# A diffusion trunk on one core: attention's low query parts on GpSimd and its normalisation per row of tiles, transposes of the experts at the ends of chunk groups, last sums in another order

## The chip, the cores and the metric

The kernel runs on one core of one Trainium2 chip. The metric is the device time of one launch in microseconds. Three runs of the kernel before gave 3383.38, 3388.33 and 3390.08 us; the median is 3388.33 us.

## What is computed

One trunk layer is applied to two groups of rows, 256 prompt rows and 1024 sample rows of width 1024, with shared weights. Cut to what matters here:

```python
def trunk_layer(x, cond, attend, ...):
    h = rmsnorm(x, norm1_g) * (1.0 + sc1) + sh1
    q, k, v, hy = jnp.split(h @ w_in, ...)
    a = attend(to_heads(q) * (HEAD_DIM ** -0.5), k, v)      # 8 heads of 64
    y_h = hyena_mixer(hy, conv_w, conv_b, k_f, hy_bias)
    mix = concat(rmsnorm(a, out_g_attn), rmsnorm(y_h, out_g_hyena)) @ w_out
    x = x + g1 * mix
    h2 = rmsnorm(x, norm2_g) * (1.0 + sc2) + sh2
    return x + g2 * expert_choice_ffn(h2, w_router, w1, w3, w2)   # 16 experts, ff 2816
y = rmsnorm(x, final_g)
```

Prompt rows attend to all 256 prompt keys. Sample rows lie on a 16 x 64 grid and attend, in one softmax, to a window of 8 x 16 neighbours with a relative bias and to 256 cached keys. Each expert takes its 128 best sample rows and its 32 best prompt rows (128 columns of 4 quarters in the second projection), computes silu(x w1) * (x w3), multiplies by w2, scales by the gate and adds the rows to x. All data is 32 bits wide.

## The kernel before, in words

The program is a row of phases, each with its own block of five engine programs written out by hand; nothing is scheduled automatically. Engines are ordered by semaphores, so the order in which each engine's code stands is the order in which it runs. The phases are filters, projection (`projection`), attention (`attention`), hyena, mixing and routing, and experts (`experts`).

**Split operands.** Matrices for samples are split in two parts, a rounded high part (ScalarE, a copy with rounding) and the rest as a low part. In attention the 64 rows of a head's queries are loaded twice, on partitions 0 to 63 and 64 to 127. ScalarE's `query_high` scales all 128 partitions by 1/8 and rounds (L802), and VectorE's `query_low` puts the rest on partitions 64 to 127 (L734). Keys are split by ScalarE (L795, L797) and GpSimd (L625, L627).

**Attention.** There are 8 heads of 10 tiles of 128 queries: tiles 0 and 1 are prompts, 2 to 9 windows, 80 tiles in all. For tile n, TensorE issues `scores(n + 1)` (L642, L646, L652), `transposes(n)` of the probabilities (L660, L669), and `values(n - 1)` (L688) into the one bank `po`. VectorE runs `add_max(n + 1)` (L746 or L748 and L750), `copy_ctx(n)` (L757), `norm(n - 1)` (a reciprocal of the sum in column 64 of `po`, L762, and a multiply, L764), and, behind tiles 6 and 7 of every head but the last, one half of the next head's `query_low`. ScalarE runs `copy_win(n)` (L820) and `exps(n + 1)` (L809, L813), and between them the high parts of the next head. `values(n)` waits for `s_norm`, that is until `norm(n - 1)` has emptied `po`. Behind the last head TensorE transposes `ar` tile by tile (`out_transposes`, L698), ScalarE and VectorE copy the banks out by turns, and two DMAs write `MIXT` (L616). ScalarE also takes the sum of squares of each tile of `ar` (`square`, L826).

**Experts.** An expert has 66 weight chunks of 512 KB. Chunks 0 to 43 (w1 and w3) make six units, five of 8 chunks and a narrow one (40 to 43); chunks 44 to 65 are w2. For each group of chunks TensorE first does `samples(c)` for every chunk of the group, with split operands and three matmuls for each product (L2806 to L2808), and then `prompts(c)` for the same chunks (L2816), in strips of 32 columns of the array. The groups end at chunks 7, 15, 23, 31, 39, 43, 51, 58 and 65. After the samples of the chunks that `TURN` names, it transposes the hidden rows of an earlier unit (L2788, L2790: six transposes, three for the last unit), and after chunk `X_TURN` the next expert's rows (L2774, L2778: ten). Two chunks later in their own loops, ScalarE and VectorE split what was transposed (`hid_hi`, L2601 and L2602, and `hid_lo`, L2670). VectorE also makes the low part of every chunk (L2500), three chunks ahead. In the last expert both engines also norm and scale the ten row tiles that only wait for their output (`bulk_square`, `bulk_first`, `bulk_scale`).

**The end.** The rows of the last expert are gathered once more, VectorE adds the last expert's output to the samples' rows `xg` and the prompts' quarters `xq`, ScalarE takes the squares, TensorE sums the quarters' squares (L2845), VectorE and ScalarE form the inverse roots, and GpSimd scatters both to `y` (L2574, L2576).

```python
    TURN = {11: 0, 19: 1, 27: 2, 35: 3, 43: 4, 47: 5}
    X_TURN = 55
```

## Time and profile before

| | us |
|---|---|
| median of three runs | 3388.33 |
| the profiled execution's own time | 3388.24 |
| its span | 3386.5 |
| TensorE busy in the span | 3194.2 (94%) |
| VectorE busy | 2191.4 (65%) |
| ScalarE busy | 1655.8 (49%) |
| GpSimd busy | 382.8 (11%) |
| attention, from the first split of keys to the last square | 680.5 to 886.9 |
| experts' matmuls | about 1336 to 3367 |

The span is the time between the first and the last instruction that the profiler saw; 1.7 us of the execution lie around it. A busy share is an average over phases with different limits, so each part of the change is read in its own stretch of the timeline.

### The profile page before, as it was taken

Reading aid. Unit: us, or ns where it says so; the run is one execution under the profiler, and the core shown is the slowest. Engines: PE = TensorE matmul, PEld = TensorE weight load, DVE = VectorE, ACT = ScalarE, POOL = GpSimd, SP = SyncE. Lnnn points to the kernel's source line nnn. Section 1 sums busy time; section 2 is a strip of 40 time slices with the busy share of each in tenths; the row PEclk is TensorE's granted clock in tenths of the full one; section 3 lists DMA queues with packets and bytes.
Section 4 is the critical chain, followed back from the end, with each engine's and each line's share of the span. In section 5 each row is a group of like instructions: output and inputs, shape, how many; then the busy total and the mean of one; then the engine's idle time right before and its main releaser. Section 6 shows DMA issues by size and latency. Waiting matters only on the chain.

```text
span 3386.5 us, 54111 instructions
## 1 busy us (share of the span) xinstructions
PE 3194.2 (94%) x22270; PEld 2430.6 (72%) x22270; DVE 2191.4 (65%) x2815; ACT 1655.8 (49%) x2156; POOL 382.8 (11%) x319
## 2 busy tenths in 40 slices
PE   5997999979899894999999999999999999999997
PEld 2443888878778773777777777777777777777775
DVE  7644233167666547777777777777777777777767
ACT  1103222156411323666666666666666666666665
POOL 2210100011244131000000000000000000000010
PEclk8998999989999896999999999999999999999999
DMA  5464432254676434788778777777777778777786
GB/s 175 170 228 177 116 115 84 73 143 127 230 245 216 149 100 162 278 297 295 272 288 294 274 288 292 275 288 290 274 290 292 275 287 295 270 289 294 275 316 247
DMA packets 226035, 791.14 MB, mean 234 GB/s; under 512 B 28526, under 2 KB 35322, under 8 KB 221565
## 3 DMA queue, kind: packets, MB, share of 16 engines
q1 hardware_dynamic: 206028, 722.02, 57.6%
q0 software_dynamic: 19760, 65.65, 6.8%
q8 instruction: 177, 2.90, 0.3%
q14 instruction: 70, 0.57, 0.0%
HBM read 730.31 MB, written 57.26 MB: 233 GB/s over the span
## 4 chain that ended last, share of the span: by engine, by line
PE 58%; DVE 1%; DMA 1%; ACT 0%; issue 0%; POOL 0%; SPq 0%; ACTq 0%; POOLq 0%; DVEq 0%
PE exp_bank L2806 15%; PE exp_bank L2808 14%; PE exp_bank L2807 14%; PE exp_bank L2816 14%; PE exp_bank L2788 1%; DMA exp_xb<-residual 1%; PE exp_bank L2790 1%; PE exp_bank L2774 0%; DMA out_y<-exp_xb 0%; DVE exp_lo L2500 0%; DVE g_pick L2367 0%; DVE g_pick L2366 0%; DVE g_pick L2369 0%; DVE exp_xb L2714 0%; DMA exp_xq<-hidden_rows,g_rows_q 0%
## 5 line engine op out<-in xcount | busy, mean ns | idle before, releaser
L2500 DVE TENSOR_TENSOR exp_lo<-exp_raw,exp_hi 128x1024 fp32r<-128x1024 f32 x1056 | 1277.8, 1223 | 249.7 <-ACT exp_hi L2496 190.8
L2496 ACT ACTIVATE exp_hi<-exp_raw 128x1024 fp32r<-128x1024 f32 x1056 | 1119.1, 1061 | 570.8 <-PE exp_bank L2808 556.7
L2806 PE MATMUL exp_bank<-exp_hi,exp_xt 128*128 128x512 f32 (+1 forms) x1536 | 588.6, 383 | 1.3 <-DVE exp_xt L2655 1.0
L2808 PE MATMUL exp_bank<-exp_hi,exp_xt 128*128 128x512 f32 (+1 forms) x1536 | 572.0, 372 | 0.0
L2807 PE MATMUL exp_bank<-exp_lo,exp_xt 128*128 128x512 f32 (+1 forms) x1536 | 571.7, 372 | 0.0
L2806 PEld LDWEIGHTS exp_bank<-exp_hi,exp_xt 128*128 128x128 f32 x1536 | 289.6, 189 | 87.0 <-issue 39.1
L2808 PEld LDWEIGHTS exp_bank<-exp_hi,exp_xt 128*128 128x128 f32 x1536 | 289.7, 189 | 51.9
L2816 PE MATMUL exp_bank<-exp_raw,exp_xtp 128*32 128x256 f32 (+1 forms) x6144 | 324.1, 363 | 0.0
L2807 PEld LDWEIGHTS exp_bank<-exp_lo,exp_xt 128*128 128x128 f32 x1536 | 290.2, 189 | 45.4
L2806 PE MATMUL exp_bank<-exp_hi,exp_hid 128*128 128x512 f32 x704 | 282.8, 402 | 0.7 <-DVE exp_lo L2500 0.7
L2816 PEld LDWEIGHTS exp_bank<-exp_raw,exp_xtp 128*32 128x32 f32 x6144 | 185.1, 110 | 127.0 <-issue 30.8
L2808 PE MATMUL exp_bank<-exp_hi,exp_hid 128*128 128x512 f32 x704 | 274.9, 390 | 0.0
L2807 PE MATMUL exp_bank<-exp_lo,exp_hid 128*128 128x512 f32 x704 | 274.3, 390 | 0.0
L503 PE MATMUL proj_bank<-proj_hh,proj_hi 128*128 128x512 f32 (+1 forms) x480 | 170.6, 355 | 2.0 <-DVE proj_lo L126 2.0
L504 PE MATMUL proj_bank<-proj_hl,proj_hi 128*128 128x512 f32 (+1 forms) x480 | 170.6, 356 | 0.0
L505 PE MATMUL proj_bank<-proj_hh,proj_lo 128*128 128x512 f32 (+1 forms) x480 | 170.5, 355 | 0.0
L2547 POOL TENSOR_TENSOR exp_step<-g_ident 1x1 f32<-1x1 f32 x16 | 4.0, 250 | 1422.8 <-PE exp_bank L2778 1391.6
L2806 PEld LDWEIGHTS exp_bank<-exp_hi,exp_hid 128*128 128x128 f32 x704 | 132.2, 188 | 42.5 <-issue 15.9
L2816 PE MATMUL exp_bank<-exp_raw,exp_hidp 128*32 128x256 f32 x2816 | 161.9, 381 | 0.0
L2808 PEld LDWEIGHTS exp_bank<-exp_hi,exp_hid 128*128 128x128 f32 x704 | 132.1, 188 | 28.6
L2807 PEld LDWEIGHTS exp_bank<-exp_lo,exp_hid 128*128 128x128 f32 x704 | 132.4, 188 | 25.2
L1180 PE MATMUL filt_pk<-filt_opnd,filt_table 128*128 128x512 f32 x292 | 140.1, 622 | 5.3 <-DVE filt_spec L1408 5.2
(413 smaller groups left out, 4299.1 us busy)
## 6 DMA issues: line engine op xcount, KB each, us to landing
exp_raw<-in_w SPq DMA_DIRECT2D x1056, 512.0 KB
hy_table<-in_basis_s POOLq DMA_DIRECT2D x64, 512.0 KB
carry_tiles<-in_w_ada SPq DMA_DIRECT2D x24, 1024.0 KB, 5.5
proj_raw<-in_w_in SPq DMA_DIRECT2D x24, 512.0 KB
filt_table<-in_kbasis_s SPq DMA_DIRECT2D x18, 512.0 KB, 6.1
spectrum_s<-filt_spec SPq DMA_DIRECT2D x34, 256.0 KB, 2.2
carry_flex<-spectrum_s SPq DMA_DIRECT2D x16, 512.0 KB
features<-proj_xr SPq DMA_DIRECT2D x12, 512.0 KB, 3.0
```

The costliest lines, as they stand in the source:

```text
L503: pe.matmul(out, whi, hh[:, k, c0:c0 + w], start=(k == 0), stop=False)
L504: pe.matmul(out, whi, hl[:, k, c0:c0 + w], start=False, stop=False)
L505: mm = pe.matmul(out, wlo, hh[:, k, c0:c0 + w], start=False, stop=(k == KT - 1))
L1180: mm = pe.matmul(pk[n % 2][:], table[:, c % NR, ti * 128:(ti + 1) * 128], opnd[:, at, x, :], start=(t == 0), stop=(t == nt - 1 and not rank1))
L2496: act.activation(st.hi[:, n % st.ns, :], raw(n), ACT.Copy).then_inc(st.hi_done, 1)
L2500: dve.tensor_tensor(st.lo[:, n % st.ns, :], raw(n), st.hi[:, n % st.ns, :].bitcast(F32), ALU.subtract).then_inc(st.lo_done, 1)
L2788: pe.transpose(turn_s[:, i * 128:(i + 1) * 128], hd[:, i * 128:(i + 1) * 128], g["ident"][:])
L2790: tr = pe.transpose(turn_p[:, i * 128:(i + 1) * 128], hdp[:, i * 128:(i + 1) * 128], g["ident"][:])
L2806: pe.matmul(out, xh, wh, start=(k == 0), stop=False)
L2807: pe.matmul(out, xh, wl, start=False, stop=False)
L2808: mm = pe.matmul(out, xl, wh, start=False, stop=(k == nk - 1))
L2816: mm = pe.matmul(banks(e * NU + i)[2][q * CAP_P:(q + 1) * CAP_P, 0:w], x[:, k, :], raw(e * NC + c)[:, base + q * w:base + q * w + w], star ...
```

## The change

In attention, the factor 1/8 moves into the projection's copies of the query blocks. VectorE's `query_low` goes, and GpSimd does the same subtraction behind its keys. `norm` becomes `copy_out`: one copy of all 65 columns of `po` into `raw_o`. In the last head, VectorE inverts the 8 sums of a tile at once and GpSimd multiplies the tile's 512 columns. The squares come one tile later. In the experts, `TURN` and `X_TURN` name the last chunks of groups. At the end, the samples' sums and squares stand ahead of the wait for the prompts' matmuls, and the inverse root is formed twice, for samples first.

```diff
@@ projection, ScalarE and VectorE
-                        ins = act.activation(to, part, ACT.Copy)
+                        ins = act.activation(to, part, ACT.Copy, scale=HD ** -0.5 if QK_ORDER[m] < 4 else 1.0)
...
+                    if QK_ORDER[m] < 4:
+                        ins = dve.tensor_scalar(to, part, HD ** -0.5, None, ALU.mult)
+                    else:
+                        ins = dve.tensor_copy(to, part)
@@ attention, GpSimd
             for h in range(NH):
                 u = h % 2
+                if h:
+                    pool.wait_ge(s_ql, 2 * h)
                 for x, (c0, c1) in enumerate(KP):
                     pool.wait_ge(s_kh, 3 * h + x + 1)
                     pool.tensor_tensor(kl[:, u, c0:c1], k[u][:, c0:c1], kh[:, u, c0:c1].bitcast(F32), ALU.subtract).then_inc(s_kl, 1)
...
+                pool.wait_ge(s_kl, 3 * h + 3)
+                for x, (c0, c1) in enumerate(KP):
+                    pool.wait_ge(s_qh, 2 * h + x + 1)
+                    out = qs[64:128, u, c0:c1]
+                    pool.tensor_tensor(out, q[u][64:128, c0:c1], out.bitcast(F32), ALU.subtract).then_inc(s_ql, 1)
+            pool.wait_ge(s_ql, 2 * NH)
+            for t in range(NTT):
+                pool.wait_ge(s_li, t + 1)
+                pool.tensor_tensor(ar[:, t, :].rearrange("p (h d) -> p h d", h=NH), raw_o[:, t, :, 0:HD],
+                                   li[:, t, :].rearrange("p (h o) -> p h o", o=1).to_broadcast([128, NH, HD]),
+                                   ALU.mult).then_inc(s_norm, 1)
@@ attention, TensorE: values(n) and out_transposes(t)
-                    pe.wait_ge(s_norm, n)
+                    pe.wait_ge(s_po, n)
...
-                pe.wait_ge(s_norm, NT - NTT + t + 1)
+                pe.wait_ge(s_norm, t + 1)
@@ attention, VectorE
-            def norm(n):
+            def copy_out(n):
                 h, t = TILES[n]
                 dve.wait_ge(s_pv, n + 1)
-                dve.reciprocal(li[:, n % 2:n % 2 + 1], po[:, HD:HV]).then_inc(s_li, 1)
-                dve.wait_ge(s_li, n + 1)
-                dve.tensor_scalar(ar[:, t, h * HD:(h + 1) * HD], po[:, 0:HD], li[:, n % 2:n % 2 + 1], None,
-                                  ALU.mult).then_inc(s_norm, 1)
+                dve.tensor_copy(raw_o[:, t, h, :], po[:, 0:HV]).then_inc(s_po, 1)
+                if h == NH - 1:
+                    dve.wait_ge(s_po, n + 1)
+                    dve.reciprocal(li[:, t, :], raw_o[:, t, :, HD]).then_inc(s_li, 1)
...
-                if h + 1 < NH and t in (6, 7):
-                    query_low(h + 1, t - 6)
@@ attention, ScalarE
-                elif t >= 2:
-                    square(t - 2)
+                elif t >= 3:
+                    square(t - 3)
@@ experts
-    TURN = {11: 0, 19: 1, 27: 2, 35: 3, 43: 4, 47: 5}
+    TURN = {15: 0, 23: 1, 31: 2, 39: 3, 43: 4, 51: 5}
...
-    X_TURN = 55
+    X_TURN = 58
@@ experts, ScalarE
-            for x in (2, 0, 1):
+            for x in range(3):
                 last_square(x)
-            act.wait_ge(s_lroot, 1)
-            act.activation(lroot[:], lr2[:], ACT.Sqrt).then_inc(s_lroot, 1)
+            for x in range(2):
+                act.wait_ge(s_lroot, 2 * x + 1)
+                act.activation(lroot[:, x:x + 1], lr2[:, x:x + 1], ACT.Sqrt).then_inc(s_lroot, 1)
@@ experts, VectorE
-            prompt_done(dve, LAST, NB)
+            done(dve, LAST, NB)
             dve.wait_ge(s_xr, 32)
             dve.wait_ge(s_bss, NTT)
-            y_part(LAST, 2).then_inc(s_lstep, 1)
             for x in range(2):
                 y_part(LAST, x).then_inc(s_lstep, 1)
-            dve.wait_ge(s_lstep, 1)
-            dve.tensor_tensor(xq[:], xq[:], yq[:], ALU.add).then_inc(s_lx, 1)
...
+            prompt_done(dve, LAST, NB)
+            y_part(LAST, 2).then_inc(s_lstep, 1)
+            dve.wait_ge(s_lstep, 3)
+            dve.tensor_tensor(xq[:], xq[:], yq[:], ALU.add).then_inc(s_lx, 1)
@@ experts, TensorE
-            pe.wait_ge(s_lss, 1)
+            pe.wait_ge(s_lss, 3)
```

VectorE in the middle of a head of attention, tiles 5 to 7, before (`attn_nc` is the context maximum, `attn_pt` the probabilities, `attn_po` the bank of values):

```order
L757 COPY attn_pt<-attn_ptc 128x256
L762 RECIPROCAL attn_li<-attn_po 128x1
L764 TENSOR_SCALAR attn_ar<-attn_po,attn_li 128x64
L734 SCALAR_TENSOR_TENSOR attn_qs<-carry_tiles,attn_qs 64x640
L748 TENSOR_REDUCE attn_nc<-attn_psc 128x1
L750 ISA attn_sw,attn_nm<-attn_psw,attn_bias,attn_nc 128x384
L750 ISA attn_nm 128x1
```

and the same place now:

```order
L766 COPY attn_pt<-attn_ptc 128x256
L771 COPY attn_raw_o<-attn_po 128x65
L757 TENSOR_REDUCE attn_nc<-attn_psc 128x1
L759 ISA attn_sw,attn_nm<-attn_psw,attn_bias,attn_nc 128x384
L759 ISA attn_nm 128x1
```

One copy stands where a reciprocal and a multiply stood, and the query rows no longer stand between one tile's output and the next tile's maximum.

TensorE in the first expert, around the transposes of the first unit's hidden rows (`exp_hd`, `exp_hdp`), before:

```order
L2807 MATMUL exp_bank<-exp_lo,exp_xt 128x512
L2808 MATMUL exp_bank<-exp_hi,exp_xt 128x512
L2788 MATMUL exp_bank<-g_ident,exp_hd 128x128 x4
L2790 MATMUL exp_bank<-g_ident,exp_hdp 128x128 x2
L2806 MATMUL exp_bank<-exp_hi,exp_xt 128x512
```

and now:

```order
L2820 MATMUL exp_bank<-exp_lo,exp_xt 128x512
L2821 MATMUL exp_bank<-exp_hi,exp_xt 128x512
L2801 MATMUL exp_bank<-g_ident,exp_hd 128x128 x4
L2803 MATMUL exp_bank<-g_ident,exp_hdp 128x128 x2
L2829 MATMUL exp_bank<-exp_raw,exp_xtp 32x256 x32
```

The transposes stood between two chunks of samples and now stand between the last chunk of samples and the prompts' matmuls of the group. Only the narrow unit's end had them there before.

VectorE at the end of the program, before (`exp_ys` and `exp_xg` are the samples' rows, `exp_yq` and `exp_xq` the prompts' quarters):

```order
L2677 SCALAR_TENSOR_TENSOR exp_yq<-exp_bank,g_gate_q,exp_row_q 128x256
L2676 SCALAR_TENSOR_TENSOR exp_ys<-exp_bank,g_gate_s,exp_row_s 128x512 x2
L2748 TENSOR_TENSOR exp_xq<-exp_xq,exp_yq 128x256
L2752 TENSOR_TENSOR exp_xg<-exp_xg,exp_ys 128x512 x2
L2755 TENSOR_TENSOR exp_lrr<-exp_lss 128x1
```

and now:

```order
L2682 SCALAR_TENSOR_TENSOR exp_ys<-exp_bank,g_gate_s,exp_row_s 128x512 x2
L2755 TENSOR_TENSOR exp_xg<-exp_xg,exp_ys 128x512 x2
L2683 SCALAR_TENSOR_TENSOR exp_yq<-exp_bank,g_gate_q,exp_row_q 128x256
L2759 TENSOR_TENSOR exp_xq<-exp_xq,exp_yq 128x256
L2769 TENSOR_TENSOR exp_lrr<-exp_lss 128x1
```

The samples' two rows stood behind the wait for the prompts' matmuls and now stand ahead of it.

## Rows read from the trace of the kernel before

**Rows 1.** Windows view, all of core 0: window, length, engines busy (instructions), PE clock, DMA.

```profile
720.00:760.00 40.00, 38.67 (x298) 34.52 (x298) 31.84 (x103) 27.05 (x56) 7.65 (x6) 1.00 0.50 133
...
1400.00:1800.00 400.00, 400.00 (x3230) 305.32 (x3230) 292.28 (x282) 252.54 (x294) 23.77 (x18) 1.00 0.77 287
```

**Rows 2.** Timeline: VectorE's copies of context columns, tiles 6 and 8, third and last head.

```profile
756.88 0.42 DVE L757 COPY attn_pt<-attn_ptc 128x256 f32<-128x256 f32 x1
...
762.57 0.42 DVE L757 COPY attn_pt<-attn_ptc 128x256 f32<-128x256 f32 x1
...
872.22 0.42 DVE L757 COPY attn_pt<-attn_ptc 128x256 f32<-128x256 f32 x1
...
876.75 0.42 DVE L757 COPY attn_pt<-attn_ptc 128x256 f32<-128x256 f32 x1
```

**Rows 3.** Timeline, third head and the turn to the fourth: start, length (us), engine, line.

```profile
755.11 0.61 ACT L813 ACTIVATE attn_p<-attn_sw,attn_nm 128x384 f32<-128x384 f32 x1
...
755.90 0.49 PE L669 MATMUL attn_ptw<-g_ident,attn_p 128*128 128x128 f32 x3
...
758.01 0.82 DVE L734 SCALAR_TENSOR_TENSOR attn_qs<-attn_q,attn_qs 64x640 fp32r<-64x640 f32 x1
...
766.00 0.63 PE L688 MATMUL attn_po<-attn_vc,attn_pt 128*128 128x65 f32 x4 [0.16 <-DVE attn_ar L764]
```

**Rows 4.** Timeline, first head's start, and GpSimd beside VectorE in the third head.

```profile
682.82 3.48 DVE L734 SCALAR_TENSOR_TENSOR attn_qs<-carry_tiles,attn_qs 64x640 fp32r<-64x640 f32 x2 [2.19 <-ACT attn_qs L802]
...
684.32 1.30 POOL L627 TENSOR_TENSOR attn_ckl<-carry_tiles,attn_ckh 128x256 fp32r<-128x256 f32 x1
...
700.30 0.74 ACT L795 ACTIVATE attn_kh<-attn_k 128x640 fp32r<-128x640 f32 x1 [6.25 <-DMA attn_bias<-in_bias]
...
751.70 1.54 POOL L625 TENSOR_TENSOR attn_kl<-attn_k,attn_kh 128x640 fp32r<-128x640 f32 x1 [0.44 <-ACT attn_kh L795]
...
751.82 0.62 DVE L750 CUSTOM_DVE_ANT_0 attn_sw<-attn_psw,carry_tiles,attn_nc 128x384 f32<-128x384 f32 x1
```

**Rows 5.** Timeline, end of attention; then the DMA view's issue row (median us to landing).

```profile
882.46 0.17 DVE L762 RECIPROCAL attn_li<-attn_po 128x1 f32<-128x1 f32 x1 [0.37 <-PE attn_po L688]
...
884.64 0.60 PE L698 MATMUL attn_psc<-g_ident,attn_ar 128*128 128x128 f32 x4
...
mixed<-attn_at SPq DMA_DIRECT2D x1, 1024.0 KB, 6.2
```

**Rows 6.** Timeline of TensorE, sixth expert: third unit, then the narrow unit's end.

```profile
2006.86 0.39 PE L2808 MATMUL exp_bank<-exp_hi,exp_xt 128*128 128x512 f32 x1
...
2009.58 0.39 PE L2808 MATMUL exp_bank<-exp_hi,exp_xt 128*128 128x512 f32 x1
...
2012.98 0.39 PE L2808 MATMUL exp_bank<-exp_hi,exp_xt 128*128 128x512 f32 x1
...
2013.30 1.07 PE L2816 MATMUL exp_bank<-exp_raw,exp_xtp 128*32 128x256 f32 x16
...
2053.94 0.38 PE L2790 MATMUL exp_bank<-g_ident,exp_hdp 128*128 128x128 f32 x2
...
2054.25 0.54 PE L2816 MATMUL exp_bank<-exp_raw,exp_xtp 128*32 128x128 f32 x12
```

**Rows 7.** Timeline of TensorE, last expert, second projection.

```profile
3349.03 0.50 PE L2806 MATMUL exp_bank<-exp_hi,exp_hid 128*128 128x512 f32 x1 [0.68 <-DVE exp_lo L2500]
```

**Rows 8.** Chain that ended last, in order of time, at the program's end.

```profile
3367.31 1.32 DVE exp_ys L2676 x2
...
3368.96 1.21 DVE exp_xg L2752 x2
...
3370.70 1.23 ACT exp_ys L2618 x4
...
3373.65 1.30 DVE exp_xg L2761
...
3377.13 0.99 POOL out_y L2576
```

More of the change, by code:

```diff
@@ L546, in attention @@
         nc0, nm = ph.sb("nc0", [128, 2]), ph.sb("nm", [128, 2])
-        li = ph.sb("li", [128, 2])
+        li = ph.sb("li", [128, NTT, NH])
+        raw_o = ph.sb("raw_o", [128, NTT, NH, HV])
         ar = ph.sb("ar", [128, NTT, DA])
@@ L727, in _ @@
             dve.memset(vc[:, :, :, HD:HV], 1.0).then_inc(s_one, 1)
-            def query_low(h, x):
-                u = h % 2
-                dve.wait_ge(s_qh, 2 * h + x + 1)
-                c0, c1 = KP[x]
-                out = qs[64:128, u, c0:c1]
-                dve.scalar_tensor_tensor(out, q[u][64:128, c0:c1], HD ** -0.5, out.bitcast(F32),
-                                         ALU.mult, ALU.subtract).then_inc(s_ql, 1)
             def add_max(n):
@@ L775, in _ @@
                 if n:
-                    norm(n - 1)
-                if h + 1 < NH and t in (6, 7):
-                    query_low(h + 1, t - 6)
+                    copy_out(n - 1)
             for t in range(1, NTT, 2):
                 if t == 5:
-                    norm(NT - 1)
+                    copy_out(NT - 1)
                 dve.wait_ge(s_tr, t + 1)
@@ L801, in query_high @@
                 c0, c1 = KP[x]
-                act.activation(qs[:, u, c0:c1], q[u][:, c0:c1], ACT.Copy, scale=HD ** -0.5).then_inc(s_qh, 1)
+                act.activation(qs[:, u, c0:c1], q[u][:, c0:c1], ACT.Copy).then_inc(s_qh, 1)
             def exps(n):
@@ L847, in _ @@
                 act.activation(at_out(t), at_in(t), ACT.Copy).then_inc(s_ata, 1)
-            for t in range(NTT - 2, NTT):
+            for t in range(NTT - 3, NTT):
                 square(t)
```

25 lines of the change are left out of this document (13 added, 12 removed).

## The prediction

> **What bounds the kernel now.** I read the windows view first. In the experts, from 1400 to 1800 us, TensorE is busy for 400.00 of 400 us at the full granted clock of 1.00 (2.4 GHz), and no other engine comes near that. In attention, from 720 to 760 us, it is busy for 38.67 of 40 us, VectorE for 31.84 and GpSimd for 7.65 [rows 1]. So the experts can only gain if TensorE's own stream gets shorter, and attention can only gain where TensorE stands still. The timeline shows where that is [rows 2, 3]. The chain of waits, last, gives the end of the program, where TensorE has finished and the other engines work in single file [rows 8]. The sum is made against the profiled execution's 3388.24 us, which is the median of the runs (3388.33) to within 0.1 us.
>
> **Attention: the query subtraction leaves VectorE.** The reader is to compare two stretches of equal work. From the copy of tile 6 to that of tile 8 it takes 762.57 - 756.88 = 5.69 us in the third head, where two halves of `query_low` of 0.82 us each [rows 3] stand between, and 876.75 - 872.22 = 4.53 us in the last head, which has none [rows 2]. The difference is 1.16 us. It is less than 1.64 because VectorE is not full. Seven heads have it: 7 x 1.16 = 8.1 us. Part of it comes back at once. Behind the last window tile the next scores are a prompt tile's: 768 columns less, at 0.227 us for 512 [rows 6] 0.34 us less, by which the transposes come earlier. In an undisturbed tile the window exponentials end at 755.72 and their transposes start at 755.90 [rows 3], 0.18 us of slack, so about 0.15 us is waited for at each turn: 7 x 0.15 = 1.0 us. Net gain 7.1 us.
>
> **Attention: one copy in place of `norm`.** In a window tile TensorE waits for nothing, so nothing is gained. At the turn from one head to the next, `values` of the last window tile waits for `norm` of the one before; TensorE starts at 766.00 behind VectorE's multiply [rows 3]. The reciprocal takes 0.17 us [rows 5]; with the handing over it adds about 0.2. A copy of 65 columns does not stand in the trace. It lies between 0.17 us (one column) and 0.42 us (256 columns, [rows 2]); I take 0.25, nearer to the one column. The wait gets shorter by 0.17 us at each of 7 turns: 1.2 us. If the copy cost 0.42, this would be nothing; if all of the wait went, 2.3 us. The waits behind it (for the maximum of the first window tile, and for its exponentials) start from TensorE's scores and stay.
>
> **Attention: the same work on GpSimd.** GpSimd takes 1.54 us for 128x640 [rows 4]. A half of 64 partitions has as many columns, so I take 1.55 us; the bounds are 0.8 (half) and 2.2. In a running head ScalarE makes the high query rows behind tiles 5 and 6. GpSimd can begin there, a tile (2.26 us) ahead of where VectorE began, and takes 0.73 us longer, so it ends 1.5 us earlier than VectorE did: nothing. At the start of the first head it is serial: cached keys from 684.32 for 0.6 to 0.8 us, then 3.1 us for the queries, about 688.2 instead of 682.82 + 3.48 = 686.30 for VectorE [rows 4]. These 1.9 us are covered: ScalarE stands still for 6.25 us until 700.30 for a DMA of the second head [rows 4], and that DMA doesn't wait for the queries. If that cover were gone, it would cost 1.9 us. The loads of the third head, which do wait for them, go out about 1 us later and leave the second head's more room: 0 to 0.7 us of gain, taken as 0.
>
> **Attention: the multiply on GpSimd.** Ten multiplies of 128x512 come with the last head. By the ratio of columns one takes 1.54 x 512 / 640 = 1.25 us; for the broadcast operand I let it be up to twice that. They come every 2.26 us, so they keep up. The last one decides: its values are there at 882.46 [rows 5]; copy, reciprocal and multiply end near 884.4. Its transposes started at 884.64, held by a bank [rows 5]. So 0, and up to 1.2 us if the multiply takes twice as long, passed straight to the DMA of 6.2 us [rows 5] that ends the phase. The three squares behind the copies end near 887.8, under that DMA. The factor 1/8 changes no instruction count in the projection, whose copies lie under matmuls: nothing, and if that cover were gone still under 0.1 us each for 12 blocks.
>
> **Experts: the transposes.** TensorE's starts tell the price. In steady samples one matmul takes (2012.98 - 2009.58) / 15 = 0.227 us. From 2006.86 to 2009.58 [rows 6] lie nine matmuls and six transposes of 0.11 us: 2.70 us without any cost of switching, against 2.72 measured. So a place in the middle of samples costs 0.02 to 0.03 us beyond the transposes themselves. Where samples turn to prompts, the start of prompts comes 0.32 us after the last sample matmul [rows 6], 0.09 more than 0.227. Where transposes stand between them, the second of the last two stands at 2054.05 and prompts start at 2054.25, 0.20 us or 0.09 more than 0.11 [rows 6]. The price of turning to strips is thus the same with and without transposes in front. The move saves only the 0.02 to 0.03: 4 x 16 of six transposes, 16 of three and 15 of ten are 95 places, and 95 x 0.025 = 2.4 us. The bounds are 0 and, if the 0.09 were hidden too, 95 x 0.11 = 10.5 us. The Trainium skill says in "TensorEngine Tiling (Array Packing)", section Key Properties, that a change of the tiling mode drains TensorE; transposes use the whole array as samples do, so by that rule no such change goes away and the sum would have 0 here instead of 2.4.
>
> **Experts: the last one.** The low part of the last unit's hidden rows is now made behind the bulk rows' root chain, not ahead of it. Just there TensorE waits for a low part of weights, 0.68 us until 3349.03 [rows 7]. ScalarE's high part and VectorE's low part, 0.6 to 0.7 us together, come on top. I take 0.7 us of loss; bounds 0 and 1.5. The other 15 experts have no such wait.
>
> **The end.** Today two output parts (1.32 us), two additions (1.21) and two squares (1.23) of the samples [rows 8] stand behind the last prompts' matmul. They now run beside the last seven chunks' matmuls for prompts, 56 records; by 16 records in 1.07 us, the last of them 0.38 long in the model [rows 6], that is about 3 us, and ScalarE's squares overlap VectorE's additions. That takes off 3.76 us. The samples' sum, scale and reciprocal steps then run beside the square of the quarters, another 0.5 us. Multiplying the samples' rows (at 3373.65) thus comes about 4.3 us earlier. The second root chain costs about 1.6 us (the joint one took 3373.65 - 3371.93 = 1.72) and the quarters' multiply some 0.5 (256 of the 1024 columns that take 1.30, and the fixed part), 2.1 us behind the first one. Today the second scatter starts at 3377.13, 2.18 us after that multiply's end at 3374.95 [rows 8], because the first scatter is issued between. So the second chain just fits under it. Gain 4.3 us; bounds 3.3 (the chain is 1 us late) and 4.8.
>
> **Sum.** -7.1 - 1.2 - 2.4 + 0.7 - 4.3 = -14.3 us, so 3388.24 - 14.3 = 3373.9; I give 3374.
>
> **Rivals.** *The transposes are worth more.* If the start of prompts were hidden behind them, the 10.5 us bound would replace 2.4: 3366. The equal 0.09 us in both rows speak against it. Chance 0.09. *GpSimd is slower than by columns, or the head's turn eats more of the gain.* With 1.2 us lost at the end of attention and only half of the 7.1 us kept: 3388.2 - 3.6 - 1.2 - 2.4 + 0.7 - 4.3 + 1.2 = 3379. The maximum, exponential and transposes are a ring behind every tile, which speaks for it; the undisturbed last head speaks against. Chance 0.15. *The move to GpSimd does not come into effect:* if the low query rows were late for each head by the 1.2 us that VectorE lost, only the end and the small terms remain: 3381. GpSimd would have to take about 3 us for each half. Chance 0.05. *GpSimd locks VectorE out; slower.* At the start, VectorE took 3.48 us for two halves of 0.82 and GpSimd 1.30 for its 256 columns [rows 4], because they ran together. If GpSimd blocked VectorE in attention too, each of 14 halves and 10 multiplies would stop it for up to 1.5 us: 14 x 1.55 + 10 x 1.25 = 34 us, less 14.3, gives 3408; from about 0.6 us for each operation on, the gain is gone. Against it: from 751.70 GpSimd worked for 1.54 us, and VectorE's operation at 751.82 took its usual 0.62 [rows 4]; it reads PSUM and one SBUF operand. The Trainium skill agrees ("SBUF — State Buffer", section Who interferes with whom): VectorE contends if it has two SBUF inputs or a two-port mode. By that rule nothing of the 34 us would come, since attention has no such operation on VectorE now; the trace at 682.82 and at 751.82 agrees. Chance 0.04.
>
> **How the numbers follow.** My forecast has 0.67. The terms at their best ends (8.1 + 2.3 + 2.4 + 0.7 + 4.8 = 18.3 us, no loss in the last expert) give 3370. All at their worst at once (half of 7.1 and 3.3 gained, 1.5 and 1.2 lost) would give 3384, but that needs four misses in one direction; the second and third rival lie at 3379 and 3381. The three runs lie within 7 us of each other, so the lower end goes to 3368. The range is 3368 to 3381; it leaves out the first and the last rival, 0.13, and the edges of the others. A measurement tells 0.2%, 6.8 us, from no change, so faster means under 3381.5: 0.87. Within 0.2%: 0.09, a part of the second and third rival. Slower: 0.04.
>
> **What would show it.** VectorE's rows in attention should be a copy of about 0.25 us in place of two instructions, and each of the first seven heads should take about 1.2 us less, end to end. TensorE's first wait of attention gets longer by about 2 us and ScalarE's wait until about 700 shorter by as much. In the experts the starts from sample to transposes to prompts should be 0.227, 0.11 and 0.20. The samples' additions should stand before the last prompts' matmul ends. A VectorE operation of attention above its old length, a GpSimd half above 2.2 us, or a TensorE wait for a low part of weights in experts 0 to 14 would prove me wrong.

## The result and the profile after

The changed kernel takes 3369.36 us (median of five runs, 3363.19 to 3372.25) beside 3383.77 us for the kernel before in the same session (3383.38 to 3390.08). The medians are 14.4 us apart. The ratio is formed from all runs: it is 0.9949, with a 95% interval of 0.9938 to 0.9959, which is 17.3 us less (13.9 to 21.0). A second session with the same kernel gave 0.9959 (0.9946 to 0.9973), 13.9 us less. The forecast was 14.3 us less. The change is faster, as predicted. The totals can't tell whether it gives more than forecast, since 14.3 lies in both intervals; the stretches below tell that attention does. One run of all that are reported here, 6212.7 us of turn_only, was in a slow state and stands in no ratio.

Single executions of one kernel differ by up to 15 us here, so the account is drawn up from the traces, stretch by stretch. Both profiled executions are used with their own time: 3388.24 us before and 3371.65 us after, 16.6 us less.

| stretch | before | after | difference | predicted |
|---|---|---|---|---|
| up to attention's first split of keys (changed only by the factor 1/8) | 680.49 | 679.81 | -0.68 | 0 |
| from there to the last copy of transposed rows | 205.47 | 196.12 | -9.35 | -8.3 |
| between attention and experts (unchanged code) | 449.96 | 449.87 | -0.09 | 0 |
| experts, first sample matmul to last prompts' matmul | 2030.83 | 2028.75 | -2.08 | -1.7 |
| from there to the end of the span | 19.70 | 15.31 | -4.39 | -4.3 |

The factor 1/8 costs nothing that shows: the projection's matmuls take 361.09 us before and 361.12 after, first start to last end.

The windows view of the changed kernel answers to [rows 1]. Its columns are window, length, and the busy time of TensorE, its weight loads, VectorE, ScalarE and GpSimd, then the granted clock and DMA:

```profile
720.00:760.00 40.00, 39.05 (x311) 35.78 (x310) 28.08 (x88) 29.04 (x59) 13.87 (x10) 1.00 0.48 122
1400.00:1800.00 400.00, 400.00 (x3288) 308.17 (x3281) 295.23 (x284) 252.18 (x297) 23.78 (x18) 1.00 0.78 288
```

In attention VectorE has gone from 31.84 to 28.08 us of 40 and GpSimd from 7.65 to 13.87. TensorE stands still 0.95 us instead of 1.33, while more heads' work goes through. In the experts TensorE is busy all the time, as before, and gets more done: 3288 matmuls instead of 3230 fall in the same 400 us (some records are missing, so this is a sign, and the periods below are the measure).

**A running head.** The timeline of VectorE in the changed kernel shows the copies of context columns. The first and last rows are tile 0 of the third and of the fourth head; the two between are tiles 6 and 8 of the third:

```profile
740.21 0.41 DVE L766 COPY attn_pt<-attn_ptc 128x256 f32<-128x256 f32 x1
...
753.90 0.42 DVE L766 COPY attn_pt<-attn_ptc 128x256 f32<-128x256 f32 x1
...
758.43 0.42 DVE L766 COPY attn_pt<-attn_ptc 128x256 f32<-128x256 f32 x1
...
761.86 0.41 DVE L766 COPY attn_pt<-attn_ptc 128x256 f32<-128x256 f32 x1
```

A head takes 761.86 - 740.21 = 21.65 us. Before, the same two copies stood in the timeline at

```profile
743.02 0.41 DVE L757 COPY attn_pt<-attn_ptc 128x256 f32<-128x256 f32 x1
...
766.10 0.42 DVE L757 COPY attn_pt<-attn_ptc 128x256 f32<-128x256 f32 x1
```

so 23.08 us: 1.4 us less for each head (1.41 on the mean of six). From tile 6 to tile 8 it now takes 758.43 - 753.90 = 4.53 us, exactly what the last head took in [rows 2].

**VectorE beside GpSimd.** GpSimd's low query half and the four VectorE instructions beside it, from the timeline of the changed kernel:

```profile
753.36 0.62 DVE L759 CUSTOM_DVE_ANT_0 attn_sw<-attn_psw,carry_tiles,attn_nc 128x384 f32<-128x384 f32 x1
753.50 1.56 POOL L638 TENSOR_TENSOR attn_qs<-attn_q,attn_qs 64x640 fp32r<-64x640 f32 x1 [1.91 <-ACT attn_qs L807]
753.90 0.08 DVE L759 DVE_READ_ACCUMULATOR2_ANT attn_nm<- 128x1 f32 x1
753.90 0.42 DVE L766 COPY attn_pt<-attn_ptc 128x256 f32<-128x256 f32 x1
754.51 0.23 DVE L771 COPY attn_raw_o<-attn_po 128x65 f32<-128x65 f32 x1 [0.19 <-PE attn_po L705]
```

The low query half takes 1.56 us on GpSimd, and the four VectorE instructions beside it have the lengths they have alone: 0.62 and 0.42 us, as in [rows 4] and [rows 2]. The copy of 65 columns takes 0.23 us.

**The start.** GpSimd's keys and queries run one behind the other, and TensorE waits for them:

```profile
680.63 3.04 POOL L631 TENSOR_TENSOR attn_kl<-carry_tiles,attn_kh 128x640 fp32r<-128x640 f32 x2 [247.30 <-ACT attn_kh L800]
...
683.64 0.71 POOL L633 TENSOR_TENSOR attn_ckl<-carry_tiles,attn_ckh 128x256 fp32r<-128x256 f32 x1
684.43 3.02 POOL L638 TENSOR_TENSOR attn_qs<-carry_tiles,attn_qs 64x640 fp32r<-64x640 f32 x2
687.50 0.29 PEld L659 LDWEIGHTS attn_psc<-attn_kh,attn_qs 128*128 128x128 f32 x1 [13.67 <-POOL attn_qs L638]
...
700.72 0.74 ACT L800 ACTIVATE attn_kh<-attn_k 128x640 fp32r<-128x640 f32 x1 [5.02 <-DMA attn_bias<-in_bias]
```

The first scores start 7.69 us after the first split of keys, against 5.86 before: 1.83 us later. ScalarE's wait for the second head's load [rows 4] is now 5.02 us instead of 6.25.

**The end of attention.** Groups of the changed kernel by line, between 673 and 876 us (busy us, mean ns of one, idle before):

```profile
L771 DVE COPY attn_raw_o<-attn_po 128x65 f32<-128x65 f32 x80 | 18.0, 224 | 29.1 <-PE attn_po L705 29.1
...
L642 POOL TENSOR_TENSOR attn_ar<-attn_raw_o,attn_li 128x512 f32<-128x512 f32 x10 | 10.4, 1045 | 19.7 <-DVE attn_li L774 19.7
```

A multiply takes 1.05 us and waits for VectorE before every one, never the other way.

**The experts.** TensorE where samples end in the sixth expert, from the timeline:

```profile
2000.87 0.39 PE L2821 MATMUL exp_bank<-exp_hi,exp_xt 128*128 128x512 f32 x1
2001.11 0.60 PE L2801 MATMUL exp_bank<-g_ident,exp_hd 128*128 128x128 f32 x4
2001.54 0.38 PE L2803 MATMUL exp_bank<-g_ident,exp_hdp 128*128 128x128 f32 x2
2001.85 1.93 PE L2829 MATMUL exp_bank<-exp_raw,exp_xtp 128*32 128x256 f32 x32
```

Prompts start 0.31 us after the first of the last two transposes, which is 0.20 after the second. That is the same as at the narrow unit's end in [rows 6]. An expert takes 126.56 us instead of 126.74.

**The end.** The chain that ended last, in order of time (start, us, what), answers to [rows 8]:

```profile
3351.39 3.20 PE exp_bank L2829 x56
...
3354.61 0.49 DVE exp_yq L2683
...
3355.13 0.43 DVE exp_xq L2759
...
3355.59 0.51 ACT exp_yq L2625 x2
...
3357.05 1.29 DVE exp_xg L2771
...
3359.84 0.49 DVE exp_xq L2775
3360.33 0.27 issue
3360.60 0.99 POOL out_y L2581
```

Ahead of the two root chains only the quarters' part, their addition and their squares stand behind the prompts' matmul now. The samples' parts and additions lie under it, in VectorE's timeline:

```profile
3351.43 1.41 DVE L2682 SCALAR_TENSOR_TENSOR exp_ys<-exp_bank,g_gate_s,exp_row_s 128x512 f32<-128x512 f32 x2 [1.93 <-PE exp_bank L2821]
3352.75 1.28 DVE L2755 TENSOR_TENSOR exp_xg<-exp_xg,exp_ys 128x512 f32<-128x512 f32 x2
```

### The profile page after: what moved, and what is told of

Same layout as the page of the kernel before. It is cut to its first block, busy times and chain, and to the rows that moved or that the text cites. A ratio compares the mean times of both kernels' runs of the same rounds, so it can differ in the third digit from the quotient of the medians.

```text
span 3369.9 us, 54074 instructions
## 1 busy us (share of the span) xinstructions
PE 3182.6 (94%) x22270; PEld 2439.4 (72%) x22270; DVE 2179.3 (65%) x2735; ACT 1657.9 (49%) x2157; POOL 417.7 (12%) x345
## 4 chain that ended last, share of the span: by engine, by line
PE 58%; DVE 1%; DMA 1%; ACT 0%; issue 0%; POOL 0%; SPq 0%; ACTq 0%; DVEq 0%
PE exp_bank L2819 15%; PE exp_bank L2821 14%; PE exp_bank L2820 14%; PE exp_bank L2829 14%; PE exp_bank L2801 1%; DMA exp_xb<-residual 1%; PE exp_bank L2803 1%; PE exp_bank L2787 0%; DMA out_y<-exp_xb 0%; DVE exp_lo L2505 0%; DVE g_pick L2372 0%; DVE g_pick L2371 0%; DVE g_pick L2374 0%; DVE exp_xb L2720 0%; ACT exp_hi L2501 0%
```

## The experiments

Twelve experiments ran. Where single runs scatter by more than the question is worth, the answer is taken from the stretch of the trace.

**attn_only**: projection and attention of the change, the experts and the end of before.

> Only the projection's scaling and attention are changed. My theory (terms add up, each in its own stretch): the part of attention gives 9 to 10 us in the trace (first split of keys to the last copy of the transposed rows), nothing else moves, 3374 to 3375 against 3384. Rival (attention's gain is partly given back later, at the phase's end or by the next phase's start): under 6 us. Rival (the later phases are worth more than their rows say): under 7 us here and over 10 in the other two runs.

Measured: 0.9968 (0.9956 to 0.9980). Attention took 196.10 us, 9.37 less than before, a head 21.65 us, an expert 126.74, the end 19.70. The theory's 9 to 10 us hold. So attention's gain is all its own, and it is 1.1 us more than the prediction's 8.3.

**turn_only**: only the places of the transposes.

```diff
-    TURN = {11: 0, 19: 1, 27: 2, 35: 3, 43: 4, 47: 5}
+    TURN = {15: 0, 23: 1, 31: 2, 39: 3, 43: 4, 51: 5}
...
-    X_TURN = 55
+    X_TURN = 58
```

> Only the places of the transposes in the experts are changed. My theory: 0.025 us for each of 95 places less 0.7 to 1.0 in the last expert, 1.5 to 2.5 us less, all between the first and the last matmul of the experts, and starts of sample, transposes and prompts at 0.227, 0.11 and 0.20 us. Rival (the turn to strips is hidden behind the transposes): 8 to 10 us less. Rival (nothing, since no change of the array's mode goes away): within 0.5 us.

Measured: 1.0002 (0.9993 to 1.0012). The total shows nothing: a gain of 2 us lies within its interval, -2.4 to 4.1 us. (In the profiled execution the first head of attention, unchanged code, took 37.56 us instead of 31.05.) The trace does show the gain: an expert takes 126.56 us instead of 126.74, and all of the experts take 1.42 us less, just under the 1.5 that the theory had as its least. If the 0.09 us of turning to strips were hidden too, an expert would have to be 0.66 us shorter (10.5 / 16). It is 0.18 shorter, so that rival is out.

**tail_only**: only the new order at the end.

> Only the order at the end is changed. My theory: 4.3 to 4.4 us less, all behind the last prompts' matmul, and the second scatter starts right behind the first. Rival (the second root chain is not hidden): 2.5 to 3.3 us less, with an idle GpSimd between the two scatters.

Measured: 0.9989 (0.9980 to 0.9998), and the end took 15.31 us instead of 19.70: all of the 4.39 us, with nothing else changed. The scatters start 1.37 us apart here too, so the part of the theory that had the second one right behind the first missed by 0.06 us.

**whole_again**: the changed kernel once more, beside the three parts.

> The changed kernel once more, on the chip and beside the runs of before of the other three. My theory: the sum of the three parts to within 1 us, 15 to 17 us less than before. Rival (the parts help one another, for instance by the granted clock or by transfers): over 2 us more than their sum.

Measured: 0.9959 (0.9946 to 0.9973), attention 195.50, end 15.32, experts 1.59 us less than before. The three parts by their stretches make 9.37 + 1.42 + 4.39 = 15.2 us, and this run shows 9.97 + 1.59 + 4.38 = 15.9: they add up to within the scatter of the first head.

**query_only** and **late_only** take attention's change apart. The first keeps the reciprocal and the multiply of every tile; the second keeps the low query halves on VectorE.

The lines that tell them apart, of query_only and then of late_only, against the kernel before; what belongs to them on GpSimd is as in the change:

```diff
-                if h + 1 < NH and t in (6, 7):
-                    query_low(h + 1, t - 6)
```

```diff
-                dve.reciprocal(li[:, n % 2:n % 2 + 1], po[:, HD:HV]).then_inc(s_li, 1)
...
+                dve.tensor_copy(raw_o[:, t, h, :], po[:, 0:HV]).then_inc(s_po, 1)
```

> Of the change only the low query rows on GpSimd, with the factor 1/8 in the projection; the reciprocal and multiply stay on VectorE. The changed kernel's heads take 21.66 us where before they took 23.07. My theory (terms as predicted): 1.0 to 1.16 of these 1.41 us for each head are this part's, heads of 21.9 to 22.1 us. Rival (both parts free the same VectorE time, so either alone gives nearly all): heads of 21.7. Rival (the copy does most): heads above 22.4.

> Of the change only the copy of 65 columns with the division in the last head; the low query rows stay on VectorE. My theory: the turn between heads gets 0.17 to 0.25 us shorter, and behind tiles 6 and 7 VectorE has 0.2 us less in each tile, so heads of 22.5 to 22.9 us; the last head's end moves by less than 0.5 us. Rival (nearly nothing alone, since the query rows hide it): 23.0. Rival (either alone gives nearly all): 21.9 or less.

Measured: 0.9974 (0.9965 to 0.9983) and 0.9984 (0.9973 to 0.9995). A head takes 21.91 us in query_only and 22.29 in late_only, against 23.07 before and 21.65 with both. The first lies at the lower edge of the 21.9 to 22.1 that its theory had, the second below the 22.5 to 22.9 of its own. The starts of `values` in the third and fourth heads of the timelines put these differences in their places (us from one tile's `values` to the next one's):

```
               tile 6 to 7   tile 7 to 8   tile 8 to 9
before              2.91          2.70          1.90
query_only          2.27          2.19          1.90
late_only           2.65          2.44          1.64
changed kernel      2.27          2.19          1.64
```

The last column is the wait of [rows 3], at the turn to the next head. Moving the query rows takes 0.64 + 0.51 = 1.15 us from the two loaded tiles and nothing at the turn. The copy alone takes 0.26 us from each of the three. With the query rows gone the first two of these were already gained, and only the turn's 0.26 is left: 1.15 + 0.26 = 1.41. The waits view of TensorE between 735 and 860 us names what went at the turn. Its columns are the line, what it waited for, us in total, times, longest. Before:

```profile
PE attn_ptc L660 <- ACT attn_p L809: 1.8, 6, 0.3
PE attn_psw L652 <- DVE attn_nm L750: 1.2, 5, 0.2
PE attn_po L688 <- DVE attn_ar L764: 1.0, 6, 0.2
```

the first of them in the timeline, at the turn to the fourth head:

```profile
763.21 0.44 PE L660 MATMUL attn_ptc<-g_ident,attn_p 128*128 128x128 f32 x2 [0.30 <-ACT attn_p L809]
```

in query_only:

```profile
PE attn_psw L662 <- DVE attn_nm L752: 1.4, 6, 0.2
PE attn_po L698 <- DVE attn_ar L766: 0.8, 5, 0.2
```

and in the changed kernel:

```profile
PE attn_psw L669 <- DVE attn_nm L759: 1.7, 6, 0.3
```

The query rows' removal takes away TensorE's wait for the probabilities (L660), the copy takes away the one for the bank of values (L688) whole. A wait for the maximum stays, as the prediction said.

**gpsimd_doubled** computes each low query half twice, first into an unused tile, to load GpSimd and to see whether that stops VectorE.

```diff
                 for x, (c0, c1) in enumerate(KP):
                     pool.wait_ge(s_qh, 2 * h + x + 1)
                     out = qs[64:128, u, c0:c1]
+                    pool.tensor_tensor(at[64:128, 0, c0:c1], q[u][64:128, c0:c1], out.bitcast(F32), ALU.subtract).then_inc(s_sp, 1)
...
```

> The changed kernel with every low query half subtracted twice on GpSimd (the first time into an unused tile): 1.55 us more for each of 16 halves. My theory (GpSimd has slack in the heads and doesn't stop VectorE): heads of 21.7 us as before, first scores 3.1 us later, under ScalarE's wait for the second head, so the phase is within 0.5 us. Rival (GpSimd locks VectorE out for what it works): up to 3 us more for each head, and longer VectorE rows. Rival (GpSimd's lateness shows at the turn): 1 us or more for each head, with TensorE waiting for GpSimd.

Measured, one run: a head takes 22.21 us, 0.55 more, where the theory had none and the rival of lateness 1 us or more. All of it comes at the turn (the copies of tiles 8 and 9 are 2.08 us apart instead of 1.24, and the next two 1.90 instead of 2.19). Its waits view, 720 to 860 us:

```profile
PEld attn_psc L662 <- POOL attn_qs L641: 4.6, 6, 0.8
```

and its timeline:

```profile
740.28 1.55 POOL L633 TENSOR_TENSOR attn_kl<-attn_k,attn_kh 128x640 fp32r<-128x640 f32 x1 [0.35 <-ACT attn_kh L803]
740.40 0.62 DVE L762 CUSTOM_DVE_ANT_0 attn_sw<-attn_psw,carry_tiles,attn_nc 128x384 f32<-128x384 f32 x1
```

VectorE's instruction under GpSimd's takes its usual 0.62 us. So do all of its kind from the second head to the end of attention: 37 of them run beside a GpSimd instruction and 19 alone, with a mean of 0.618 us for both. So GpSimd doesn't lock VectorE out here; that rival is refuted. What GpSimd does cost is being late: with twice the query work TensorE waits up to 0.8 us for it at each turn. In the changed kernel itself there is no such wait after the first head. The time of this run, 3367.09 us, is no measure of the added work, because its first head took 22.50 us.

**last_unit_old_place** and **last_expert_old** are to find the loss in the last expert. In the first, the last expert's last unit is transposed at chunk 47 again; in the second, all six units of the last expert are at their old places.

The other 15 experts keep `TURN`; in last_expert_old the new line reads {11: 0, 19: 1, 27: 2, 35: 3, 43: 4, 47: 5}.

```diff
     TURN = {15: 0, 23: 1, 31: 2, 39: 3, 43: 4, 51: 5}
+    TURN_L = {15: 0, 23: 1, 31: 2, 39: 3, 43: 4, 47: 5}
...
-                        if c in TURN:
+                        if c in turn(e):
```

> The changed kernel, but in the last expert the last unit's transposes stand behind chunk 47 again. My theory (the loss in the last expert, 128.9 us against 127.9, is this unit's low part behind the root chain): 0.7 to 1.0 us back. Rival (it comes from the earlier moved units, whose low parts now meet the first bulk group): under 0.2 us back, and the long gaps of TensorE around chunks 29 and 38 stay.

> The changed kernel, but in the last expert all transposes stand at their old places (chunks 11, 19, 27, 35, 43, 47). The last expert took 126.9 to 128.2 us with the old places in five profiles and 128.6 to 129.2 with the new ones. Theory (the moved splits meet the bulk groups' root chains, in several places): 127 to 128.2 us, about 1 us less than in the changed kernel. Rival (the spread comes from the bulk rows' transfers alone): again 128.6 to 129.2.

Measured, one run each: 3370.72 and 3367.79 us; the last expert took 128.23 and 127.36 us. Over the other traces, the last expert took 126.94, 127.26, 127.36, 127.65, 127.94, 128.00 and 128.23 us where all its transposes stood at the old places, and 128.63, 128.72, 128.82, 128.92 and 129.18 at the new ones. The two sets don't overlap; their means are 1.2 us apart. The waits view of TensorE from 3236 to 3366 us tells what it waits for. Before:

```profile
PE exp_bank L2806 <- DVE exp_lo L2500: 0.9, 2, 0.7
```

and the changed kernel:

```profile
PE exp_bank L2819 <- DVE exp_lo L2505: 1.9, 3, 0.9
```

So the loss of 1.0 us is waiting for low parts of weights. The longest waits stand in the timeline of TensorE, changed kernel:

```profile
3296.67 0.50 PE L2819 MATMUL exp_bank<-exp_hi,exp_xt 128*128 128x512 f32 x1 [0.94 <-DVE exp_lo L2505]
...
3336.82 0.50 PE L2819 MATMUL exp_bank<-exp_hi,exp_hid 128*128 128x512 f32 x1 [0.68 <-DVE exp_lo L2505]
```

The wait in the second projection, where the prediction put the loss, is the same 0.68 us as in [rows 7]. The 0.94 us stand at a sample chunk of the first projection, where the longest such wait before was 0.25 us. Single waits move about between traces (with all transposes at the old places, last_expert_old has one of 0.73 us in the first projection and one_tile_later one of 0.82), so the two projections are compared as a whole, over all fourteen traces. The last expert's time from its first sample matmul to the first of the second projection, and from there to the end:

| places of the transposes in the last expert | traces | first projection, us | second projection, us |
|---|---|---|---|
| all old | 8 | 85.72 to 86.22 | 41.15 to 42.22 |
| last unit old, others new (last_unit_old_place) | 1 | 86.93 | 41.30 |
| all new | 5 | 86.75 to 87.19 | 41.59 to 42.07 |

The first projection tells the places apart without overlap, by 1.0 us on the means, and last_unit_old_place stands with the new ones. So the loss of about 1 us comes with the earlier units' new places, and putting the last unit back doesn't remove it. The second projection varies by 1.1 us with its places unchanged, so the 0.7 us that last_unit_old_place gained in it (41.30 against 42.02) may be chance: a price of the last unit's place is neither shown nor excluded. How an earlier unit costs time is seen in one place. In the changed kernel VectorE's low part of hidden rows stands in a full stretch, just ahead of the first bulk group's root chain and of the low part of weights for which TensorE waits until 3296.67:

```profile
3290.19 0.69 DVE L2676 TENSOR_TENSOR exp_hid<-exp_bank,exp_hid 128x512 fp32r<-128x512 f32 x1
```

In last_expert_old the same part stands at 3282.56, behind 2.50 us in which VectorE had nothing to do. The low part of weights in question also waits 0.61 us for ScalarE's high part, at 3295.39, so ScalarE has a share in it. That this is the whole mechanism is not shown.

**first_head_later**, **both** and **one_tile_later** try to use ScalarE's wait in the first head. ScalarE is held there because the second head's keys come late and `keys_high(1)` stands behind tiles 2 to 4. The first moves keys and queries of the second head to later tiles, both adds last_expert_old, and one_tile_later goes less far, with last_expert_old too.

```diff
-                if h + 1 < NH:
+                if h == 0:
+                    if t == 5:
+                        keys_high(1, 0)
+                    if t == 6:
+                        keys_high(1, 1)
+                        keys_high(1, 2)
+                    if t in (7, 8):
+                        query_high(1, t - 7)
+                elif h + 1 < NH:
                     if t in (2, 3, 4):
```

In one_tile_later the tests read 4, 5 and (6, 7), with t - 6.

> The changed kernel, but in the first head ScalarE takes the next head's keys behind tiles 5 and 6 and its queries behind 7 and 8, instead of 2 to 4 and 5 to 6, so that its own exponentials don't stand behind the wait for the second head's transfer. Theory (TensorE's long gap in the first head is ScalarE's wait, and later heads don't need it): first head 22 to 24 us instead of 27.9 to 28.5, 4 to 6 us less in all. Rival (the wait only moves, to the second head's first scores): first and second head together as before, under 1.5 us gained.

> Both of the two others at once. Theory (they add up): 5 to 6 us less than the changed kernel, near 3363 where before has 3384, ratio 0.993 to 0.995. Rival (one of them gives nothing): within 2 us of the changed kernel.

> The changed kernel with the last expert's transposes at their old places, and in the first head the second head's keys behind tiles 4 and 5 and its queries behind 6 and 7 (one tile earlier than in the run before, two later than in the changed kernel). Theory (in the run before GpSimd's chain for the second head ended about 3.4 us too late; one tile of 2.26 us earlier leaves about 1.2): first and second head together about 47.5 us instead of 49.7, the last expert 127.4 to 128.2, in all 3 to 3.5 us less than the changed kernel, and this is the version to keep. Rival (the second head's transfer sets the start of its second tile whatever ScalarE does): 49.5 again, only the 1 us of the last expert left.

Measured: first_head_later 0.9941 (0.9928 to 0.9955), both 0.9950 (0.9936 to 0.9963), one_tile_later 0.9934 (0.9921 to 0.9948), with a median of 3359.99 us beside 3385.14. The gains of 4 to 6 and of 5 to 6 us over the changed kernel that the first two were expected to have did not come. In first_head_later the first two heads took 26.47 + 23.34 = 49.81 us, about as in the changed kernel (28.50 + 21.66 = 50.16): the wait moved to the second head's start, where the timeline has

```profile
717.39 0.58 PE L659 MATMUL attn_psc<-attn_kh,attn_qs 128*128 128x256 f32 x1 [2.81 <-POOL attn_qs L638]
```

GpSimd, now the last link for the queries, was late. In one_tile_later ScalarE doesn't wait for the load at all, the wait for GpSimd is 0.56 us (at 705.46), and the two heads take 22.14 + 21.65 = 43.79 us, where 47.5 was expected. Windows view of the changed kernel, then of one_tile_later, same columns as above:

```profile
697.00:704.00 7.00, 2.76 (x17) 2.22 (x15) 1.70 (x5) 2.92 (x6) 2.15 (x2) 0.77 0.87 175
704.00:712.00 8.00, 8.00 (x54) 7.83 (x54) 3.60 (x12) 5.11 (x12) 3.23 (x3) 0.77 0.01 6
```

```profile
697.00:704.00 7.00, 7.00 (x62) 6.88 (x60) 5.05 (x16) 6.58 (x15) 5.49 (x5) 1.00 0.34 69
704.00:712.00 8.00, 7.17 (x56) 6.29 (x54) 4.68 (x16) 3.57 (x8) 1.40 (x1) 1.00 0.85 263
```

TensorE stood still for 4.24 us of the first stretch in the changed kernel. The mean granted clock of 0.77 hides the two levels: in windows of 2 us it is 1.00 (2.4 GHz) until 700, 0.50 (1.2 GHz) from 702 to 706, and 1.00 again from 708, behind a standstill of TensorE from 698 to 702. From 704 to 706 10 matmuls lie, from 708 to 710 20. So the hole costs its own length and then the slow stretch behind it. one_tile_later is the best version tried. Five profiles of the changed attention gave 27.9 to 28.5 us for its first head, so 22.14 is no chance value of the same thing; but it is one profile. gpsimd_doubled, whose scores start 3 us later, came to 22.50 without this edit, and the intervals of the totals overlap (0.9921 to 0.9948 against 0.9938 to 0.9959). That every run saves 6 us is not shown.

## What of the prediction held, and which steps failed

The direction and the parts were right: every part gained in its own stretch, and no rival came true. Three steps of the sum failed. "About 0.15 us is waited for at each turn" took 1.0 us off attention, and the runs show 0. "The wait gets shorter by 0.17 us at each of 7 turns" is 0.26. The loss in the last expert was put on the last unit's low part in the second projection, and lies in the first projection, with the earlier units' new places. The first two make the gain too small, and the base of the sum, 3388.24 us, was above what the kernel before mostly takes; each is taken up below.

**Query rows off VectorE: 1.16 us right, the give-back wrong.** The prediction took 1.16 us for a head from [rows 2] and gave 0.15 back, because the scores behind the last window tile are shorter and the slack before the exponentials is only 0.18 us. query_only shows 23.07 - 21.91 = 1.16 us, the whole of it. VectorE's copies show a reaction that is not kept: in query_only those of tiles 8 and 9 stand 1.34 us apart instead of 1.12 (0.22 us given back), and from there to tile 0 of the next head it is 2.19 instead of 2.41 (0.22 us regained). TensorE shows none: the step of `values` from tile 8 to 9 is 1.90 us in both. The kernel before already waited at the turn, 0.30 us for probabilities (at 763.21, above), and that wait is gone in query_only. The step "about 0.15 us is waited for at each turn" fails in that it set a new wait against a turn that it took to be free of waits for probabilities.

**The copy: 0.26 us at a turn, not 0.17.** The copy takes 0.224 us where 0.25 was taken. The pair that it replaces stood at the turn of [rows 3] as

```profile
765.36 0.17 DVE L762 RECIPROCAL attn_li<-attn_po 128x1 f32<-128x1 f32 x1 [1.25 <-PE attn_po L688]
765.57 0.28 DVE L764 TENSOR_SCALAR attn_ar<-attn_po,attn_li 128x64 f32<-128x64 f32 x1
```

and took 765.57 + 0.28 - 765.36 = 0.49 us from start to end. The copy is 0.26 us shorter, and TensorE's wait is gone altogether. The prediction's upper bound, that all of the wait goes, was the right case; it priced it at 2.3 us for seven turns, and it is 1.8.

Together 7 x (0.15 + 0.09) = 1.7 us were missed. In the profiled execution 1.1 of them show. The six heads from the second on give 8.5 us; the first head and its late start together give 0.7 where 1.4 was there to be had, and the end of attention 0.1. The first head depends on when the second head's load lands, which was 1.1 us later against the first split in the profile after.

**GpSimd.** A half takes 1.55 us as priced, with 64 partitions as with 128, and the multiply 1.05 where 1.25 was taken, so the last one hid as said. The late start of the scores was priced at 1.9 us and is 1.83. It hides under ScalarE's wait, as said, which fell from 6.25 to 5.02 us although the load that ends it came 1.1 us later against the first split. The end of attention needed no term. The rival that GpSimd locks VectorE out found no support in any row, with twice the load either. The rival "half the gain" stands against 1.41 us a head.

**Transposes.** Priced at 0.025 us for each of 95 places, 2.4 us; measured 0.18 us for each of experts 1 to 14, 0.03 for each of the six places in one. Turning to strips costs the same 0.09 us behind transposes as behind samples. As a sign of being wrong the prediction named a TensorE wait for a low part of weights in experts 0 to 14. Between 1330 and 3230 us no matmul has one, but 13 weight loads wait for one, up to 0.4 us, where before none did. The experts' period gets shorter all the same. In "TensorEngine Tiling (Array Packing)", section Key Properties, the Trainium skill has a mode change drain TensorE. By that rule alone these moves would give nothing, since none takes a mode change away; the 0.18 us is small, but it repeats to 0.01 in every expert of every trace that has the new places.

**The last expert.** Priced at 0.7 us of loss by the last unit's low part; measured about 1.0 in the profiled execution (127.94 to 128.92). The size nearly holds, by luck, and the step fails in its place: the wait of [rows 7] did not grow, and the first projection got 1.0 us longer wherever the earlier units stood at their new places, to which the prediction gave nothing. It had looked at one wait of one trace. In the other four traces with all places old in every expert, that wait in the second projection is 0.67 us (attn_only), 0.51 us (tail_only) and missing twice (query_only, late_only).

**The end.** Priced at 4.3 us, measured 4.39. The second chain was to fit just under the first scatter: it ends at 3360.33. GpSimd's timeline shows that it was just not in time:

```profile
3359.23 1.00 POOL L2579 DMA_INDIRECT out_y<-exp_xg,g_rows_s  x1 [0.53 <-issue]
3360.60 0.99 POOL L2581 DMA_INDIRECT out_y<-exp_xq,g_rows_q  x1 [0.37 <-DVE exp_xq L2775]
```

The second scatter waits for the quarters and starts 1.37 us after the first, 0.06 us more than before.

**The time.** The differences have one sign: 1.05 us in attention, 0.38 in the experts, 0.09 at the end, 0.09 between attention and experts and 0.68 ahead of attention make 16.6 instead of 14.3. The last two are chance, and the experts' 0.38 can be: their stretch takes 2029.87 to 2031.27 us in the five traces with all places old and 2028.51 to 2029.41 in the five with all new, 1.6 us less on the means, where 1.7 was forecast. A second reason is the base. The profiled execution and the three runs of the kernel before lay in the upper part of what it does: in the four later sessions its medians were 3383.1 to 3386.5 us, not 3388.3. A gain of 17.3 us from 3383.77 is 3366.5 us, under the lower end of the range, although the median of the runs, 3369.36, lies in it. The range held 7 us of run scatter in words, but left only 2 us below its own best case for it.

## What to carry to other kernels

In a ring of engines, where each waits for the next tile after tile, a wait that appears behind an edit is a loss only if the same point of the next period is still late by it; here 0.22 us were given back at one tile and regained at the next. Two edits that empty the same engine in the same tile don't add up (1.16 and 0.78 us alone, 1.41 together), so take each tile of the ring by itself and ask which wait ends last after both. A hole in TensorE's work is priced with the slow stretch behind it, and here the cure was to move the waiting instructions by one or two tiles, not as far as possible: one tile more, and they were late for the next consumer.

## What the hardware did that was not expected

- GpSimd's multiply of 512 columns with a broadcast operand takes 1.05 us, its subtraction of 640 columns 1.55 us and of 256 columns 0.71 to 0.73: 2.0, 2.4 and 2.8 ns a column. The broadcast operand doesn't make it dearer than the subtractions. A subtraction on 64 partitions takes as long as one on 128.
- The first head of attention took 31.05, 31.30 and 37.56 us in three profiles of the same attention code, while the six heads behind it agree within 0.05 us in each of the three. ScalarE's wait for the second head's load was 6.25, 6.41 and 8.74 us in them. Attention's first split of keys came between 671.2 and 685.6 us over all fourteen traces. A change worth 3 us can't be read from a few totals of this kernel. Its stretch can: the heads behind the first repeat to 0.06 us and the end of the program to 0.02, but attention as a whole differed by 0.6 us between two profiles of the changed kernel, and the last expert by 1.3.
- A profile with more work in it showed a shorter stretch: with the low query halves computed twice, attention's first scores came 3.0 us later against the first split (10.66 instead of 7.69 us), and the first head took 22.50 instead of 28.50 us, where TensorE met no hole between 697 and 704 us and had a granted clock of 1.00. ScalarE didn't wait for the second head's load there at all (5.02 us in the changed kernel). It is one profile; that the later start was the cause was not tested.
